# Values of the sparse attention: the product turned round, with a copy and three transposes behind it

## The reference, cut to what matters

```python
kv = (rmsnorm(c_kv, kv_norm) @ w_ukv).reshape(b, t, A_HEADS, 2 * A_HEAD_DIM)
k, v = kv[..., :A_HEAD_DIM], kv[..., A_HEAD_DIM:]
...
logits = jnp.einsum('bqhd,bqkhd->bqhk', q_b, k_sel).astype(jnp.float32) * scale
...
p = jax.nn.softmax(logits, axis=-1).astype(v.dtype)
return jnp.einsum('bqhk,bqkhd->bqhd', p, v_sel)
```

## Time and profile before

| what | value |
|---|---|
| median of 3 runs | 3031.74 us (3031.32 to 3034.64) |
| the profiled execution's own time | 3032.98 us |
| its span | 3031.2 us, 62062 instructions |
| PE busy | 2997.3 us (99%), 24197 matmuls |
| PEld, DVE, ACT, POOL busy | 97%, 56%, 45%, 5% |
| chain that ended last | PE 92%, DVE 4%, ACT 2%, issue 1%, DMA 1% |

### The profile page before, as it was taken

One profiled execution on the slowest core, in us unless ns is written; L12 is line 12 of the kernel. 1 busy time (PEld: TensorE's weight loads), 2 busy tenths in 40 slices (PEclk: granted clock), 3 DMA queues, 4 the chain that ended last, 5 costly groups with the idle time before them and its releaser, 6 DMA issues.

```text
span 3031.2 us, 62062 instructions
## 1 busy us (share of the span) xinstructions
PE 2997.3 (99%) x24197; PEld 2941.8 (97%) x24197; DVE 1699.5 (56%) x2466; ACT 1368.8 (45%) x2026; POOL 166.2 (5%) x174
## 2 busy tenths in 40 slices
PE   9999999999999999999999999999999999999998
PEld 9879998999999999999999999999999999999998
DVE  4887675575554455545555555554456555455545
ACT  5545555553333333345444444444454443344443
POOL 0011110000000000000010111110000000000000
PEclk9999999999999999999999999999999999999999
DMA  5222222434445545455444444444545555555554
GB/s 203 98 69 102 96 91 94 155 144 170 176 164 175 185 170 178 162 171 169 156 167 159 159 155 164 163 156 167 194 153 180 181 186 179 190 185 188 182 179 153
DMA packets 77521, 482.54 MB, mean 159 GB/s; under 512 B 8949, under 2 KB 11381, under 8 KB 32640
## 3 DMA queue, kind: packets, MB, share of 16 engines
q1 hardware_dynamic: 77376, 481.21, 45.2%
q0 software_dynamic: 64, 0.21, 0.0%
HBM read 479.29 MB, written 2.10 MB: 159 GB/s over the span
## 4 chain that ended last, share of the span: by engine, by line
PE 92%; DVE 4%; ACT 2%; issue 1%; DMA 1%; DVEq 0%; ACTq 0%; SPq 0%
PE ps L453 91%; DVE w_lo L1760 1%; DVE bias L1987 0%; ACT w_hi L1140 0%; PE ps L1074 0%; DMA raw<-in_w_heads 0%; DVE w_lo L1874 0%; DVE ret_sq L2374 0%; DVE u L2370 0%; DVE bias L2001 0%; PE ps L688 0%; ACT mid_hi L1697 0%; DVE u L1824 0%; DMA h<-in_x_t 0%; ACT x_hi L1200 0%
## 5 line engine op out<-in xcount | busy, mean ns | idle before, releaser
L453 PE MATMUL ps<-x_hi,w_hi 128*128 128x272 f32 (+1 forms) x4992 | 1446.8, 290 | 1.9 <-ACT x_hi L1200 0.8
L453 PE MATMUL ps<-x_lo,w_hi 128*128 128x272 f32 (+1 forms) x4992 | 1434.3, 287 | 0.3 <-DVE x_lo L1817 0.3
L453 PE MATMUL ps<-x_hi,w_lo 128*128 128x272 f32 (+1 forms) x4992 | 1426.0, 286 | 0.0
L1760 DVE TENSOR_TENSOR w_lo<-raw,w_hi 128x1024 fp32r<-128x1024 f32 (+2 forms) x952 | 1031.7, 1123 | 366.0 <-ACT w_hi L1140 353.9
L1140 ACT ACTIVATE w_hi<-raw 128x1024 fp32r<-128x1024 f32 (+1 forms) x902 | 849.6, 972 | 485.7 <-PE ps L453 397.2
L453 PEld LDWEIGHTS ps<-x_hi,w_hi 128*128 128x128 f32 x4992 | 941.8, 189 | 19.3 <-issue 14.6
L453 PEld LDWEIGHTS ps<-x_lo,w_hi 128*128 128x128 f32 x4992 | 939.5, 188 | 3.3 <-DVE x_lo L1817 1.0
L453 PEld LDWEIGHTS ps<-x_hi,w_lo 128*128 128x128 f32 x4992 | 941.9, 189 | 0.4
L453 PE MATMUL ps<-mid_hi,w_lo 128*128 128x256 f32 (+1 forms) x1920 | 543.8, 283 | 0.0
L453 PE MATMUL ps<-mid_hi,w_hi 128*128 128x256 f32 (+1 forms) x1920 | 543.5, 283 | 0.0
L453 PE MATMUL ps<-mid_lo,w_hi 128*128 128x256 f32 (+1 forms) x1920 | 543.1, 283 | 0.0
(11 more groups left out here) (264 smaller groups left out, 2193.2 us busy)
## 6 DMA issues: line engine op xcount, KB each, us to landing
raw<-in_w_up SPq DMA_DIRECT2D x176, 1024.0 KB, 4.8
raw<-in_w_ret_in SPq DMA_DIRECT2D x96, 1024.0 KB, 4.8
raw<-in_w_down SPq DMA_DIRECT2D x128, 704.0 KB, 4.1
raw<-in_w_heads SPq DMA_DIRECT2D x32, 1024.0 KB, 4.8
raw<-in_w_ret_out SPq DMA_DIRECT2D x32, 1024.0 KB, 4.8
raw<-in_w_mix_early SPq DMA_DIRECT2D x16, 768.0 KB, 4.4
raw<-in_w_latent SPq DMA_DIRECT2D x8, 1024.0 KB, 4.8
raw<-in_w_dsa SPq DMA_DIRECT2D x16, 256.0 KB, 2.5
```

The source lines that it names most:

```text
L453: return nc.tensor.matmul(o, lhs, rhs, start=start, stop=stop)
L1760: V.tensor_tensor(w_lo[:, slot, cut], raw[:, slot, cut], w_hi[:, slot, cut], ALU.subtract).then_inc(lo_ready, count)
```

## The change

The values are made like the keys, with the weights stationary and all 272 tokens moving: 6 matmuls of 272 columns into `BK_D0`. ACT copies that to `p_t` (`dsa_vt`), TensorE turns it in three transposes into bank `BK_D1` (`dsa_vturn`), and ACT copies the result to `v_h` in two instructions (`dsa_values`). `ckv_hi` and `ckv_lo` lose their columns of zeros, and POOL the two memsets. In head 7 `dsa_logits` stands four blocks of `mix(8, ...)` later than before.

```diff
@@ dsa_kv on TensorE
-                for b in range(3):
-                    o = ps[:, BK_D0, b * P:(b + 1) * P]
-                    for k in range(2):
-                        xh, xl = ckv_hi[:, k, b * P:(b + 1) * P], ckv_lo[:, k, b * P:(b + 1) * P]
-                        wh, wl = w_hi[:, 1, (2 + k) * P:(3 + k) * P], w_lo[:, 1, (2 + k) * P:(3 + k) * P]
-                        mm(o, xh, wh, k == 0, False)
-                        mm(o, xl, wh, False, False)
-                        last = mm(o, xh, wl, False, k == 1)
-                last.then_inc(products, 1)
+                multiply(ps[:, BK_D0, 0:T], 1, 2, 2, lambda k: ckv_hi[:, k, 0:T], lambda k: ckv_lo[:, k, 0:T]
+                         ).then_inc(products, 1)
+
+            def dsa_vturn(i):
+                pe.wait_ge(DA.sem, DA.after("vt", i))
+                for b, (q0, n) in enumerate(BLK):
+                    last = nc.tensor.transpose(ps[0:n, BK_D1, b * P:(b + 1) * P], p_t[:, q0:q0 + n], ident[:])
+                last.then_inc(DP.sem, 1)
@@ mixer_body on TensorE
                 if not first:
                     gdn_sums(g)
                     gdn_spread(g, f)
+                if d is not None:
+                    dsa_vturn(d)
@@ heads 5, 6, 7 on TensorE
             gdn_spread(g, g - 1)
+            dsa_vturn(5)
...
             mix(4, 0, 4)
+            dsa_vturn(6)
...
             mix(8, 0, 4)
+            dsa_vturn(7)
+            mix(8, 4, 8)
             dsa_logits(7)
-            mix(8, 4, 12)
+            mix(8, 8, 12)
@@ ScalarE
+            def dsa_vt(i):
+                act.wait_ge(products, dsa_at(i)[1] + 3)
+                nc.scalar.activation(p_t[:, 0:T], ps[:, BK_D0, 0:T], ACT.Copy).then_inc(DA.sem, 1)
+
             def dsa_values(i):
-                act.wait_ge(products, dsa_at(i)[1] + 3)
-                nc.scalar.activation(v_h[:].rearrange("p b t -> p (b t)"), ps[:, BK_D0, 0:3 * P], ACT.Copy
-                                     ).then_inc(DA.sem, 1)
+                act.wait_ge(DP.sem, DP.after("vturned", i))
+                nc.scalar.activation(v_h[:, 0:2].rearrange("p b t -> p (b t)"), ps[:, BK_D1, 0:2 * P], ACT.Copy)
+                nc.scalar.activation(v_h[0:16, 2], ps[0:16, BK_D1, 2 * P:3 * P], ACT.Copy).then_inc(DA.sem, 1)
@@ mixer_body on ScalarE
                 if f is not None:
                     out_ln(f)
+                if d is not None:
+                    dsa_vt(d)
                 if g is not None:
                     gdn_ln(g)
```

More of the change, by code:

```diff
@@ L180, in trunk @@
             cq_lo = sb("cq_lo", [P, 4, T], F32R, first)
-            ckv_hi = sb("ckv_hi", [P, 2, 3 * P], F32R, first)
-            ckv_lo = sb("ckv_lo", [P, 2, 3 * P], F32R, first)
+            ckv_hi = sb("ckv_hi", [P, 2, T], F32R, first)
+            ckv_lo = sb("ckv_lo", [P, 2, T], F32R, first)
             kidx = sb("kidx", [P, T], F32, first)
@@ L301, in trunk @@
         CA = Steps(sem("conv_act"), "silu0 silu1 silu2 gate")
-        DP = Steps(sem("dsa_pe"), "logits turned attended")
+        DP = Steps(sem("dsa_pe"), "vturned logits turned attended")
         DV = Steps(sem("dsa_dve"), "scored maxed recips y_lo")
-        DA = Steps(sem("dsa_act"), "values exped probs turned y_hi")
+        DA = Steps(sem("dsa_act"), "vt values exped probs turned y_hi")
         GP = Steps(sem("gdn_pe"), "sums spread scores turned tm0 "
@@ L1576, in _ @@
             out_ln(g - 1)
+            dsa_vt(5)
             gdn_ln(g)
@@ L1599, in _ @@
             gdn_y(g, 4)
+            dsa_vt(6)
             split_last("mix4", EARLY_W, (1,))
@@ L1621, in _ @@
             split_last("mix8", EARLY_W)
+            dsa_vt(7)
             dsa_values(7)
@@ L2443, in _ @@
             G.memset(scratch[:], 1.0)
-            G.memset(ckv_hi[:, :, T:3 * P].bitcast(F32), 0.0)
-            G.memset(ckv_lo[:, :, T:3 * P].bitcast(F32), 0.0)
             G.memset(conv_in[:, :, 0:3], 0.0)
```

## The result

| what | before | after |
|---|---|---|
| median of 10 runs each, side by side | 3031.71 us (3029.23 to 3036.26) | 3038.86 us (3037.34 to 3043.24) |
| ratio | | 1.0021, 95% interval 1.0013 to 1.0029 |
| profiled execution's own time, its span | 3032.98, 3031.2 us | 3037.37, 3035.6 us |
| mean granted clock of the profiled execution | 0.997 | 0.995 |

The account below looks back on a forecast made before the run. TensorE was busy 99%, but its next steps were taken to wait for ACT, a DMA or DVE. Terms +0.6 + 0.15 - 0.3 + 0.33 + 1.8 = +2.6 us gave 3034.3 us, range 3030 to 3038.

Parts of the forecast that it names:

- rival B: In the rounds, new idle time ahead of the spread lowers the clock, 1.7 us a fall, 8.4 in five; chance 0.07.
- the 1.21 us: Per head, TensorE time saved by 6 wide matmuls replacing 18 narrow ones, before transposes and if nothing waits.
- the 1.8 and 2.4 us waits of heads 6 and 7: Behind dsa_kv, TensorE's waits grow from 0.59 to 1.8 in head 6 and from 1.25 to 2.4 in head 7.
- head 7's +1.8: Later logits at the lower clock delay DVE's w_lo of mix9, so TensorE starts mix9 1.8 us later.
- the wait for mix9 of "near 1.6": In head 7, a new TensorE wait near 1.6 us ahead of mix9, released by DVE's w_lo.
- head 6's transposes: In head 6 the saving goes into a longer wait and the transposes come later, +0.33 us.
- The estimate of 0.83 for three transposes: Cost per head by the Trainium skill's 275 ns for one transpose; the prediction rejected it for the trace's 0.33 us.
- Terms of +0.31, +0.31 and 3 x 0.05: Rounds one and two each lose 0.31 us to transposes; rounds three to five each lose 0.05 after small gains.
- Head 5's -0.3: In head 5 earlier sums let gdn_ln start some 0.4 us earlier, less 0.1 for the copy pair: -0.3 us.
- Rival A: Waits at the spread and in heads 6 and 7 move forward, so all eight heads gain, -7.0 us; chance 0.04.
- Rival C: In head 7 the clock stays up and the new wait doesn't come, so the sum is +1.2 us; chance 0.24.

Follow-up runs that it names:

- warm_fill: Changed kernel plus unread float32 matmuls between sums and spread, four in each round, two in head 5; 3036.32 us, ratio 1.0009.
- warm_dve: Changed kernel plus those unread matmuls ahead of the spread and, on DVE, mix9's w_lo ahead of dsa_score(7); 3033.60 us, ratio 1.0004.
- early_all: Changed kernel with values' copies and transposes moved ahead of the delta rule's normalization in rounds and head 5, and early in heads 6 and 7; 3038.28 us, ratio 1.0015.
- dve_first: Changed kernel with one swap on DVE, the w_lo of mix9 ahead of dsa_score(7); 3038.66 us, ratio 1.0017.
- warm_behind: Changed kernel plus the same unread matmuls, four in a round, two in head 5, but behind the spread; 3044.05 us, ratio 1.0039.
- early_values: Changed kernel with values' copies ahead of out_ln and transposes right behind dsa_kv, in rounds and head 5 only; 3043.76 us, ratio 1.0036.
- no_turn: Changed kernel without the copy to p_t and the transposes, v_h filled in the wrong layout; 3037.95 us, ratio 1.0016.
- real_fill: Changed kernel with due work ahead of the spread: three blocks of part in each round, two of mix0 in head 5; 3034.65 us, ratio 1.0008.

## Why the prediction was wrong, step by step

**The step that failed** is that the sum put falls of the clock in the rounds and in head 6 at nothing, and gave rival B, "The clock falls in the rounds", 0.07. The runs show four falls more than before, at 1.47 each, 5.9 of the 7.1 us; with the waits ahead of the spreads filled (warm_fill) all four are gone, head 6's too though its own wait stayed, and with head 7's order mended besides (warm_dve) nothing is left that can be told from zero.

The mechanism was written down with nearly the right price (1.7 a fall) and then put aside by two arguments. The first was one observation, that the clock stayed at 1.00 behind the 1.40 of head 5: one place of the trace where a wait did not lower the clock was taken for a rule. That place is still so after the change (1.41 there, clock 1.00), while 1.08 at another place lowered it in two rounds of four and 1.37 in round one; and in early_all the same wait at the same place does stand in a stretch of 0.53. The second was that the narrow matmuls around head 7's idle time are gone now; the falls came without them. Nor had I let B reach head 6, whose wait of 1.87 was forecast and whose clock fell too.

B's own number for three rounds, 2.6 + 3 x 1.7 = 7.7, comes close to the 7.1, but partly by luck: there were four falls, not three, and the rest of the sum was +1.2 (7.1 - 5.9) and not +2.6. My +2.6 with four falls at 1.47 would have been 8.5.

**Right:** the spread follows `out_ln` and nothing of the 1.21 us is saved in the rounds (the waits of 1.08 and more at L1461 show it); 72 matmuls fewer; three transposes in 0.30; logits without a wait; the 1.8 and 2.4 us waits of heads 6 and 7 (1.87, 2.44); head 7's +1.8 (+1.82), with the wait for mix9 of "near 1.6" (1.46), released by DVE and gone when DVE's order was swapped (dve_first); head 6's transposes (+0.33; 1.88 less a fall of 1.47 is +0.41). The estimate of 0.83 for three transposes took a single one's duration three times; in the third round after, each lasts 0.27 to 0.35, but they start 0.16 and 0.11 apart, so they overlap, and going by the trace's 0.33 for all three was right.

**Mis-sized:** the rounds without falls. Terms of +0.31, +0.31 and 3 x 0.05 stood there, +0.75; measured, 3.18 less three falls is -1.2, and warm_fill, free of falls, gives 245.29 - 246.44 = -1.15. Of this -0.44 belongs to head 5, so the rounds themselves gained 0.8: all take 49.13 without a fall, and took 49.32, 49.12, 49.33, 49.33 and 49.34 before. Two things were missing. The spread's wait in rounds one and two was put to `out_ln` as such, but ACT's chain was late there because of a transfer. The row of the split in the second round before, and then after:

```profile
274.71 2.01 ACT L1140 ACTIVATE w_hi<-raw 128x1024 fp32r<-128x1024 f32 x2 [1.14 <-DMA raw<-in_w_heads]
```

```profile
276.06 2.01 ACT L1145 ACTIVATE w_hi<-raw 128x1024 fp32r<-128x1024 f32 x2 [0.81 <-PE ps L453]
```

And of the 0.29 us by which the work stands later behind the second spread, 0.13 are gone at the delta rule's L745: it stood 11.22 behind the spread before and 11.38 after, with the place for its predecessor (L738) at 8.49 and 8.77. That is a wait for DVE too short to be listed, of the kind that I had looked for at the logits only. In warm_fill's third round, against before, it is 0.17. Head 5's -0.3 was near: its spread comes after 48.69 where a round takes 49.13, -0.44, and the logits start 3.69 behind it, 3.63 before.

**Rival A** (the saving is real) is out, by every spread's wait. **Rival C** (clock stays up in head 7) did not come: 0.83 in the window of head 7.

**Open:** why the clock fell in two to four of five like rounds and not in all, and which of the work before the wait counts. Head 6 above all is open: TensorE waits there for 1.77 to 1.87 us in eight of the profiled kernels, and the clock fell behind it in three (the changed kernel, warm_behind, early_values) and not in five (warm_fill, warm_dve, dve_first, no_turn, real_fill), though no edit touched that wait. No run here fills or removes it alone. So the wait alone doesn't decide.

## What to carry to other kernels

Work taken off an engine that is busy 99% was worth nothing here where its next step followed another engine's chain within 0.1 us, and it can cost more than nothing, because TensorE's clock may fall behind the new idle time (here in three of five like places). Before such a saving is counted, price the fall, count the places where the new idle time stands, and give them more weight than one place where nothing happened; if the idle time can't be filled with useful work, a few unused matmuls in it can be cheaper than the fall (3.6 us back here by the ratios, 5.9 in the traces). And look at what an order does behind a wait: the logits right behind their operands, with the copies that they need moved forward too, gave 2 to 3.5 us without any change of the arithmetic.

## What the hardware showed that I had not expected

- A wait of 1.08 to 1.37 us between plain float32 matmuls of `ones` is followed by a granted clock of 0.5 in three of five rounds (50.60 us instead of 49.13), in four with dve_first and in two with no_turn; one of 0.86 (round one) or 0.19 (rounds two to five) in warm_fill in none, and one of 0.49 ahead of the transposes (early_values) in none. One of 1.40 ahead of L745 stands in a stretch at 0.5 in early_all and not in early_values or in the changed kernel.
- While the clock is down, matmuls of 272 columns start 0.226 us apart (331.35 to 331.57) instead of 0.126, and the slow stretch goes on after the wait: in the third round until 334.04, behind the transposes and 15 matmuls or so. That is what makes a fall dearer than the wait ahead of it. The Trainium skill ("TensorE: Matmul & The Clock Gate", Part 1: A second HAM failure mode) says of another kernel that frequent short idle times between groups of matmuls make the clock swing between its levels and that this costs throughput between the groups, while the usual matmul still runs at the full clock. This case agrees in that: waits of 1.08 us were followed by falls of 1.47 us each. Here the price lies in the matmuls right behind the wait.
- The same three transposes take 0.30 us at the full clock and 0.50 in head 7, where it is down (556.94 to 557.44).
